# VectorE's order inside a slot of prompt attention: low half before score chunk

## The reference, cut to what matters

```
def block(args):                       # one block of 128 queries
    s = einsum('bqhd,bkhd->bhqk', q, K) * scale
    s = s + fq[..., None] - fk
    s = where(k_pos <= q_pos, s, -inf)
    p = softmax(s, axis=-1)
    return einsum('bhqk,bkhd->bqhd', p, V)
...
b = o.reshape(B, T, D_ATT) * silu(ag)  # the gate of the attention branch
```

## Time and profile before

| | |
|---|---|
| time before, median of 3 runs | 1635.46 us (1633.32 to 1637.83) |
| the profiled execution's own time | 1640.0 us |
| its span in the trace | 1638.0 us |
| its mean granted TensorE clock | 0.974 of full speed |
| busy over the span: PE, PEld | 94%, 83% |
| busy over the span: DVE, ACT, POOL | 50%, 39%, 25% |

### The profile page before, as it was taken

How to read it: one execution, slowest core, us unless ns; L and a number is a source line. 1 busy time by engine, 2 the same in 40 slices (tenths; PEclk the granted TensorE clock), 3 DMA queues, 4 the chain that set the end, 5 groups by cost and what they waited for, 6 DMA issues and landing times. The chain is left out here.

```text
span 1638.0 us, 24621 instructions
## 1 busy us (share of the span) xinstructions
PE 1545.1 (94%) x9264; PEld 1364.5 (83%) x9264; DVE 823.0 (50%) x2069; ACT 632.5 (39%) x1347; POOL 409.6 (25%) x706
## 2 busy tenths in 40 slices
PE   6999999999999899999999999999987999599999
PEld 6997888878899898998888888888875777478887
DVE  3332112232534323216898888888875788342221
ACT  4443020110211101016787887787763344121000
POOL 1110005555300000114344444444313443100000
PEclk9999999999999899999999999999997999789999
DMA  5433122121200201402223323313107664254341
GB/s 152 147 106 92 47 85 75 45 96 46 84 25 20 63 19 39 87 15 59 61 49 77 70 49 69 69 46 70 29 14 249 208 223 150 100 206 141 130 155 64
DMA packets 181510, 144.63 MB, mean 88 GB/s; under 512 B 104015, under 2 KB 140784, under 8 KB 181392
## 3 DMA queue, kind: packets, MB, share of 16 engines
q1 hardware_dynamic: 178880, 134.08, 28.0%
q10 hardware_dynamic: 2448, 8.91, 1.3%
q0 software_dynamic: 64, 0.07, 0.1%
HBM read 106.50 MB, written 36.53 MB: 87 GB/s over the span
## 5 line engine op out<-in xcount | busy, mean ns | idle before, releaser
L937 PE MATMUL banks<-in_w_hi,in_xt_hi 128*128 128x512 f32 (+1 forms) x680 | 242.3, 356 | 4.8 <-DVE in_w_lo L667 3.4
L937 PE MATMUL banks<-in_w_hi,in_xt_lo 128*128 128x512 f32 (+1 forms) x680 | 239.9, 353 | 0.0
L937 PE MATMUL banks<-in_w_lo,in_xt_hi 128*128 128x512 f32 (+1 forms) x680 | 239.1, 352 | 0.0
L1440 DVE CUSTOM_DVE_ANT_0 pa_s_ring<-banks,pa_f_b 128x512 f32<-128x512 f32 (+2 forms) x320 | 193.1, 603 | 34.8 <-PE banks L1541 31.9
L943 PE MATMUL banks<-in_xt_hi,in_w_hi 128*128 128x384 f32 (+1 forms) x576 | 196.8, 342 | 8.1 <-DVE in_w_lo L667 7.9
L1488 DVE TENSOR_TENSOR pa_pt_lo<-banks,pa_pt_hi 128x512 fp32r<-128x512 f32 (+2 forms) x320 | 192.9, 606 | 21.5 <-ACT pa_pt_hi L1419 18.9
L943 PE MATMUL banks<-in_xt_hi,in_w_lo 128*128 128x384 f32 (+1 forms) x576 | 192.1, 333 | 0.0
L943 PE MATMUL banks<-in_xt_lo,in_w_hi 128*128 128x384 f32 (+1 forms) x576 | 191.9, 333 | 0.0
L1419 ACT ACTIVATE pa_pt_hi<-banks 128x512 fp32r<-128x512 f32 (+2 forms) x320 | 166.9, 535 | 53.8 <-PE banks L1550 52.6
L1550 PE MATMUL banks<-ident,pa_s_ring 128*128 128x128 f32 x1088 | 174.0, 275 | 9.6 <-DVE pa_pt_lo L1488 4.0
L1566 PE MATMUL banks<-pa_pt_hi,pa_vs 128*128 128x256 f32 x576 | 163.7, 300 | 0.4 <-DVE pa_parts L1468 0.3
(11 more groups left out here) (245 smaller groups left out, 2831.1 us busy)
## 6 DMA issues: line engine op xcount, KB each, us to landing
sa_k_c<-in_cache_k_dram SPq DMA_DIRECT2D x8, 2048.0 KB, 10.0
sa_v_c<-in_cache_v_dram SPq DMA_DIRECT2D x8, 2048.0 KB, 8.5
in_w_raw<-in_w_in_dram SPq DMA_DIRECT2D x48, 256.0 KB, 3.6
out_dram<-in_out SPq DMA_DIRECT2D x34, 256.0 KB, 2.0
out_dram<-op_y ACTq DMA_DIRECT2D x17, 512.0 KB, 4.9
in_x<-in_x_prompt_dram SPq DMA_DIRECT2D x16, 512.0 KB, 3.5
op_x<-in_x_prompt_dram SPq DMA_DIRECT2D x16, 512.0 KB, 4.8
pa_f_b<-scratch_f SPq DMA_DIRECT2D x28, 256.0 KB, 5.1
```

The lines of the kernel that those rows point to most:

```text
L937: mm = pe.matmul(ps[:, u % NBANK, 0:n], tile_of(xa, t)[:, k, :], wa[:, k, c0:c0 + n], start=(k == 0 and q == 0), stop=(k == KT - 1 and q = ...
L1440: done = dve.tensor_tensor_reduce(scores_of(j)[:, b * P:(b + nb) * P], ps_s[:, (h * NQD + at) % 3, 0:nb * P], f_b[h % 2][:, b * P:(b + nb) ...
```

## The change

In each slot, VectorE's list had the take of tile j + 3's chunk n first and the low half of tile j's chunk n second. The change exchanges the two. What follows them in the slot (inverted sums, gate) stays behind both.

```diff
                 for n in range(slots):
-                    if n < n_take:
-                        take_chunk(*nxt, n)
                     if n < len(banks):
                         b, nb = banks[n]
                         dve.wait_ge(hi_done, h * NQD + q_before(j) + n + 1)
...
                                           pt_hi[g % 2][:, b:b + nb, cols].bitcast(F32),
                                           ALU.subtract).then_inc(lo_done, 1)
+                    if n < n_take:
+                        take_chunk(*nxt, n)
                     if n == 0 and j % 2 == 0 and (j or h):
                         invert_sums(*((h, j - 1) if j else (h - 1, NJ - 1)))
                     if n == min(1, slots - 1) and j % 2 == 1:
```

## The result

The changed kernel took 1639.91 us, median of 12 runs (1637.80 to 1643.58), against 1636.15 us for the kernel before (12 runs, 1633.32 to 1637.99). The ratio is 1.0025 with a 95% interval of 1.0016 to 1.0034: slower by about 4 us, a quarter of a per cent, and clear of no change.

A forecast was written before the change was run, and what follows sets the result against it. TensorE sets the pace in the prompt attention (463.1 of 479 us busy). Tile 5's 2.1, tile 3's 1.3, tile 7's 0.3 and the last head's 0.5 sum to 4.2 us on 1635.46: 1639.7 us, range 1633 to 1644.

The forecast's parts named there:

- Low halves earlier are worth 0: VectorE's low halves, one place earlier in the list, save TensorE nothing: value taken 0, bounds 0 and −6.0 us.
- Tile 5, 0.22 to 0.31 in each head, 0.26 taken: Tile 5's later gate delays tile 6's first product by 0.22 to 0.31 us in 8 heads: 2.1 us.
- Tile 3, 0.26 in five heads and 0 in heads 4 and 5: Tile 3's gate comes 0.22 to 0.30 us later, all lost at the first product in five heads: 1.3 us.
- Tile 7, 0.25 to 0.34, of which tile 9 swallows 0.25: Tile 7's later gate delays the product; tile 9's stall leaves 0 to 0.09 us, 0.3 us for seven heads.
- The chain that I named: Tile 8's first transpose, ScalarE's high half, exponential, next high half, then the low half setting tile 9's 0.25 us stall.
- The last head, 0.5 for tile 7: The last head has no preps and no swallowing stall, so tile 7's whole delay counts there: 0.5 us.
- the second rival: Slower, twice as much: scores of tiles 9 and 10 wait for later takes in seven heads; 1642.5 us, chance 0.17.
- my signs of being wrong: Scores begin waiting for takes, low-half waits fall, or first products of tiles 4 and 6 start no later.
- The tightest score: Score needing the bank of the take behind tile 9's gate: still in time by about 0.2 us, cost 0.
- the faster one: Rival: banks come free sooner, TensorE's 17 low-half waits (6.0 us) go; 1632.5 or 1629.5 us, chance 0.12.
- tile 8's stall: Argument against the faster rival: the waiting transpose stands behind a low half that started with ScalarE's release.
- The rival with no change: First products are delayed but TensorE's later waits absorb it: 0 to 1 us, 1635.5 to 1636.5 us, chance 0.21.

The follow-up runs named there:

- The first experiment: Changed kernel with the gate put ahead of the take, behind the low half: 1632.90 against 1635.51 us for the kernel before, ratio 0.9992.

## Why the prediction was right

- *Low halves earlier are worth 0.* Right, to 0.1 us a head. TensorE's waits for them are 6.0 us before and 5.9 after. The first experiment and the one with low half first and an early gate confirm it by the time. The 320 slots in which the prediction lets two instructions trade places are all low halves; only 245 of them share a slot with a take. The other 75 are in tiles 13 to 15, where all 17 waits are, which is why none of them moved.
- *The gate behind the take is the cost.* Right, and shown by removal: with the gate ahead of the take the loss is gone.
- *Tile 5, 0.22 to 0.31 in each head, 0.26 taken.* Measured 0.31. The term was a little small: the delay of the first product was right (0.25), but its successor is late too, by a further 0.07 us at tile 6 and 0.10 at tile 8, which the sum did not have.
- *Tile 3, 0.26 in five heads and 0 in heads 4 and 5.* Measured 0.22 in the five heads, about 0 in head 4 and under 0.1 in head 5. Of the 0.22, 0.12 already comes at the prep of tile 4 in four of the five (the last head has no preps): its split by GpSimd waits behind the inverted sums, which the change puts behind a take as well. I had left that road out, at nothing and without a reason; TensorE's waits for that split grew from 1.8 us (3 times) to 3.2 (7 times). Behind it the gate's wait is shorter by as much, so the sum is the same. That it is the same is luck.
- *Tile 7, 0.25 to 0.34, of which tile 9 swallows 0.25.* Measured 0.37 and 0.29, 0.06 to 0.08 left, where I took 0.05. The chain that I named holds: the low half ends last ahead of the stall.
- *The last head, 0.5 for tile 7.* Measured 0.49, and 1.22 us for the whole head where the terms gave 1.0. The difference is the 0.2 us of scores that wait for takes, the second rival's mechanism, in the one head in which I had not looked for it. It was also one of my signs of being wrong, and it did appear, though small and in this head only.
- *The tightest score, in time by about 0.2 us in head 4.* There the take's read ended at 1019.29 and the score started at 1019.55: 0.26.
- *Sum.* 4.2 us forecast, 4.65 measured in the stretch, and 0.25% of the launch's time, about 4.1 us. Tile 3 was a little below its term, the other terms a little above.
- *Range and chances.* The range of 1633 to 1644 would have held no change as well, so it tests little; the forecast's own 1638.9 to 1641.1 is the sharper statement, and 1639.91 lies in it. A difference under 4.9 us I had called hard to tell from none. With twelve runs of each kernel the interval, 1.0016 to 1.0034, does tell it.

Of the rivals, the faster one rested on the 17 waits for low halves. They are in tiles 13 to 15, out of the exchange's reach, and my argument against that rival, from tile 8's stall, was about another place. Seven of them were indeed late by their place in VectorE's list, but behind tile 13's gate and not behind a take: moving that gate took 0.41 us a head away. The rival with no change had its absorbing stall, but only for the one delay whose chain runs beside it; the slower one appears in the last head alone.

The rule of the Trainium skill (VectorE: DVE Perf Modes, The DRAIN you can't avoid) that would have added 0.1 us per gate did not show: in the changed kernel the starts of 0.68 and 0.69 us instructions are again 0.60 to 0.61 apart (1000.97, 1001.58), and two takes in a row are too:

```profile
936.49 0.68 DVE L1440 CUSTOM_DVE_ANT_0 pa_s_ring<-banks,pa_f_b 128x512 f32<-128x512 f32 x1
...
937.10 0.55 DVE L1440 CUSTOM_DVE_ANT_0 pa_s_ring<-banks,pa_f_b 128x384 f32<-128x384 f32 x1
```

## What to carry to other kernels

When two instructions of an in-order engine trade places, look less at the two than at what stands right behind the pair: it inherits the wait of whichever is last released. For each late step ask whether the next stall of the bounding engine has a chain that runs past the step (then it swallows the delay) or through it (then it does not). A small consumer in a slot, such as the gate here, whose inputs are ready early, is better off in front of the instruction that waits, where it fills idle time. And find out in which tiles the waits of a table lie before a gain or a rival is built on their sum.

## What was not expected of the hardware

- A product whose weight load was released late delays its successor too: in the changed kernel they start 0.23 us apart instead of 0.12.
- Exchanging the pair in odd tiles only cost 9.5 us of stretch, in all tiles 4.65, in even tiles 1.7, of which 1.0 is a slow transfer.
- The same 512 KB transfer, issued at the same point of a head, took 7.6 us to land in one execution and 8.6 in another.
- The spans of two profiled executions agreed to 0.1 us while the stretch under study differed by 4.65 us.
